# Norms on a row per head, another engine order and another transfer order ahead of a chunked recurrence

## The reference

```python
kk = heads(zk * k_k)
kk = kk / jnp.maximum(jnp.sqrt(jnp.sum(kk * kk, axis=-1, keepdims=True)), 1e-12)
k = zk * (1.0 + (a - 1.0) * k_a)
def step(state, inp):
    r_t, d_t, k_t, v_t, kk_t, a_t = inp
    sa = jnp.einsum('bhij,bhj->bhi', state, -kk_t)
    state = (state * d_t[:, :, None, :] + sa[..., None] * (kk_t * a_t)[:, :, None, :]
             + v_t[..., None] * k_t[:, :, None, :])
    return state, jnp.einsum('bhij,bhj->bhi', state, r_t)
...
mean = jnp.mean(y, axis=-1, keepdims=True)
var = jnp.mean(jnp.square(y - mean), axis=-1, keepdims=True)
y = ((y - mean) * lax.rsqrt(var + GN_EPS)).reshape(B, S, H * N)
```

## Time and profile before

| what | us |
|---|---|
| median of 3 runs | 1891.51 |
| lowest and highest run | 1888.94, 1892.16 |
| the profiled execution | 1893.17 |
| its span | 1891.4 |
| TensorE busy | 1767.9 |
| VectorE busy | 1201.5 |
| ScalarE busy | 791.1 |
| GpSimd busy | 178.5 |

### The profile page before, as it was taken

How to read it: one execution, slowest core, us unless ns; L and a number is a source line. 1 busy time by engine, 2 the same in 40 slices (tenths; PEclk the granted TensorE clock), 3 DMA queues, 4 the chain that set the end, 5 groups by cost and what they waited for, 6 DMA issues and landing times.

```text
span 1891.4 us, 29535 instructions
## 1 busy us (share of the span) xinstructions
PE 1767.9 (93%) x12770; PEld 1629.6 (86%) x12770; DVE 1201.5 (64%) x1828; ACT 791.1 (42%) x1131; POOL 178.5 (9%) x72
## 2 busy tenths in 40 slices
PE   6979979889989899999999999999999998999997
PEld 5869867789989899998898888888899898987897
DVE  5775665664688648875444998555575455555664
ACT  4624432434444432234443222444434545454553
POOL 0200321000555720000000000000000000000000
PEclk8889976899999999999999999999999998999999
DMA  9414232244435443335554333555654333443330
GB/s 380 178 67 166 103 112 94 107 156 156 157 137 198 157 155 113 112 112 191 187 179 156 112 112 112 200 190 189 249 180 165 128 144 129 150 151 126 112 112 23
DMA packets 40452, 281.70 MB, mean 149 GB/s; under 512 B 4481, under 2 KB 4865, under 8 KB 7938
## 3 DMA queue, kind: packets, MB, share of 16 engines
q1 hardware_dynamic: 40034, 279.66, 41.1%
q10 hardware_dynamic: 288, 0.15, 0.0%
HBM read 278.75 MB, written 1.05 MB: 148 GB/s over the span
## 4 chain that ended last, share of the span: by engine, by line
PE 81%; DVE 12%; ACT 3%; POOL 2%; DMA 1%; issue 1%; ACTq 0%; SPq 0%; DVEq 0%
PE ps L549 80%; POOL WL L2486 2%; DVE WL L1743 1%; DVE ar L1716 1%; DVE ar L2199 1%; DVE ar L1735 1%; DVE ar L2196 1%; DMA ar<-in_in_g 1%; ACT WH L1196 1%; ACT ar L1188 1%; DVE ar L2203 1%; DVE ar L2018 1%; DVE ar L1727 1%; DMA vec<-in_vec 0%; DVE ar L1892 0%
## 5 line engine op out<-in xcount | busy, mean ns | idle before, releaser
L549 PE MATMUL ps<-RH,WH 128*128 128x256 f32 x2520 | 745.5, 296 | 47.1 <-DVE WL L1743 16.1
L549 PE MATMUL ps<-RL,WH 128*128 128x256 f32 x2520 | 724.4, 287 | 0.0
L549 PE MATMUL ps<-RH,WL 128*128 128x256 f32 x2520 | 723.6, 287 | 0.0
L1743 DVE TENSOR_TENSOR WL<-ar,WH 128x1024 fp32r<-128x1024 f32 (+1 forms) x410 | 482.4, 1209 | 361.0 <-ACT WH L1196 360.8
L1196 ACT ACTIVATE WH<-ar 128x1024 fp32r<-128x1024 f32 (+1 forms) x478 | 480.1, 1040 | 308.2 <-PE ps L549 271.3
L549 PEld LDWEIGHTS ps<-RH,WH 128*128 128x128 f32 x2520 | 495.4, 197 | 62.3 <-issue 19.1
L549 PEld LDWEIGHTS ps<-RL,WH 128*128 128x128 f32 x2520 | 496.0, 197 | 2.9 <-issue 2.4
L549 PEld LDWEIGHTS ps<-RH,WL 128*128 128x128 f32 x2520 | 495.0, 196 | 0.0
L549 PE MATMUL ps<-ar 128*128 128x64 f32 (+10 forms) x2700 | 325.4, 300 | 33.9 <-DVE ar L1731 10.0
L549 PEld LDWEIGHTS ps<-ar 128*128 128x128 f32 (+6 forms) x2700 | 279.3, 185 | 75.1 <-issue 39.9
L549 PE MATMUL ps<-WH,RH 128*128 128x512 f32 (+1 forms) x704 | 262.5, 373 | 19.5 <-DVE WL L1743 12.7
(11 more groups left out here) (146 smaller groups left out, 1022.5 us busy)
## 6 DMA issues: line engine op xcount, KB each, us to landing
ar<-in_u SPq DMA_DIRECT2D x64, 1024.0 KB, 4.8
ar<-in_v SPq DMA_DIRECT2D x64, 1024.0 KB, 4.8
ar<-in_adr SPq DMA_DIRECT2D x16, 1024.0 KB, 4.8
ar<-in_ada SPq DMA_DIRECT2D x8, 1024.0 KB, 12.5
ar<-in_in_g SPq DMA_DIRECT2D x8, 1024.0 KB, 7.2
ar<-in_wq SPq DMA_DIRECT2D x8, 1024.0 KB, 4.8
ar<-in_a_qk SPq DMA_DIRECT2D x8, 1024.0 KB, 6.8
ar<-in_a_v SPq DMA_DIRECT2D x8, 1024.0 KB, 4.8
```

Source lines behind the costliest of these rows:

```text
L549: ins = q.matmul(o, l, r, start=start and i == 0, stop=stop and i == len(pairs) - 1, skip_group_check=skip)
L1743: q.tensor_tensor(l[:, x:z, :], src[:, x:z, :], h[:, x:z, :].bitcast(F32), ALU.subtract).then_inc(*v.up(("lo", n, i)))
```

## The change

1. **Norms on a row per head.** `head_sums` replaces `blksum` for kk and `y_sum` for the variance: for tile k the weights are every fourth column of `blk`, so the sums come out on 32 partitions, 32k to 32k + 31, the first 16 for one head, the other 16 for the other. All eight heads then lie in one tile of 128 x 256 (128 x 128 for half of the output). Bound, root and reciprocal work on that tile. `spread` then brings each head's number back to its 64 rows: a matmul with 32 rows of a new constant, two of them side by side in two waves, with a wait for the first wave. The products that apply the inverse read it from PSUM.
2. **Order of VectorE and ScalarE ahead of the solves.** The products with `k_k` on `al` come first, the norm's steps are taken apart and stand between the chunks' low halves, the key factors on ScalarE come after the root, sine and cosine move from there into the solves (steps 2 and 6 of the first half, with VectorE's part at step 4), the products by the inverse come after the first value chunks' low halves.
3. **Low halves** of `in_rkv` 4 and 5 are VectorE's.
4. **Transfers.** `dma_order` sorts the chunks from `in_v` 0 to `adr` 15 by when their slot comes free, in terms of the position of the chunk that holds it; `adr` chunks count as later. Slots stay as they were.

```diff
+def dma_order():
+    lo, hi = CHUNKS.index(("in_v", 0)), CHUNKS.index(("adr", 15)) + 1
+    def free(c):
+        return chunk_before(c) + (0.5 if CHUNKS[c][0] == "adr" else -1.5)
+    return list(range(lo)) + sorted(range(lo, hi), key=free) + list(range(hi, len(CHUNKS)))
...
-    return name == "in_g" or name == "in_rkv" and j >= 4 or name == "u" and j < 32 and j % 4 != 3
+    return name == "in_g" or name == "u" and j < 32 and j % 4 != 3
...
+    def head_sums(o, src, ts, need):
+        p.wait_ge(*on(need))
+        for k in range(4):
+            ins = mm(o[32 * k:32 * k + 32, 0:ts.stop - ts.start], [(blk[:, 0:P:4], src[:, k, ts])])
+        return ins
+    def spread(tag, rows, need):
+        w = rows.shape[1]
+        banks = [bank((tag, f)) for f in range(0, 4, 2)]
+        p.wait_ge(*on(need))
+        for g in range(2):
+            if g == 1:
+                p.wait_ge(*p.last())
+            for f, o in zip(range(0, 4, 2), banks):
+                s = slice(32 * (f + g), 32 * (f + g) + 32)
+                mm(o[:, g * w:(g + 1) * w], [(cst("spread")[s, :], rows[s, :])]).then_inc(*p.up((tag, f)))
...
-        blksum("kk norm", m.SQ, "kk squared")
+        head_sums(bank("kk norm"), m.SQ, slice(0, T), "kk squared").then_inc(*p.up("kk norm"))
+        some(zs, 8)
+        spread("kk inverse", m.kk, "kk inverses")
         finish(zs)
...
             if i == 11:
-                y_sum("y var", 0, m.Ysq, ("y squared", 0))
+                y_var(0)
+            if i == 13:
+                spread(("y inverse", 0), m.Yrt[0], ("y inverses", 0))
...
         some(steps, 2)
-        y_sum("y var", 1, m.Ysq, ("y squared", 1))
+        y_var(1)
+        some(steps, 4)
+        spread(("y inverse", 1), m.Yrt[1], ("y inverses", 1))
```

More of the change, by code:

```diff
@@ L1877, in front, with keyed @@
         some(zs, 7)
-        Bt, zr, zk = m.Bt, m.rd, m.zk
-        some(zs, 4)
-        for f in range(2):
-            t = ("kk norm", f)
-            v.wait_ge(*on(t))
-            q.tensor_scalar(flat(m.RN)[:, f * 512:(f + 1) * 512], tile(t), 1e-24, None, ALU.max).then_inc(*v.up("kk norm2"))
-            v.mark(("out", t))
+        zr, zk = m.rd, m.zk
+        some(zs, 3)
+        def keyed(x):
+            v.wait_ge(*v.last())
+            for k in range(4):
+                q.scalar_tensor_tensor(x[:, k, :], zk[:, k, :], vc("k_k", k), x[:, k, :], ALU.mult, ALU.mult).then_inc(*v.up())
+        v.wait_ge(*on("kk norm"))
+        TS(m.kk, tile("kk norm")[:, 0:T], 1e-24, None, ALU.max, None, "kk norm2")
+        v.mark(("out", "kk norm"))
+        v.wait_ge(*on(("out", ("sums before", 2))))
+        keyed(m.al)
+        some(zs, 2)
+        v.wait_ge(*on("kk norms"))
+        REC(m.kk, m.kk, "kk inverses")
+        some(zs, 4)
         v.wait_ge(*on("key factors"))
@@ L2615, in constants @@
     put("mask3", np.concatenate([tri, np.zeros((P, P)), tri], 1))
+    put("spread", row % 32 == col // 64 * 16)
     put("iota", col * np.ones((P, 1)))
```

75 lines of the change are left out of this document (44 added, 31 removed).

## The result

| | runs | median, us | lowest, highest |
|---|---|---|---|
| before | 4 | 1891.51 | 1888.94, 1892.16 |
| changed | 4 | 1875.63 | 1872.92, 1877.93 |

The ratio is 0.9918, with a 95% interval of 0.9901 to 0.9935: 15.9 us less, where 22.1 were forecast (1869.4, range 1858 to 1880). The profiled execution took 1876.42 (span 1874.6) against 1893.17 (1891.4): 16.8 us between the two traces. Direction and range held; most terms of the sum did not.

A forecast was written before the change was run, and what follows sets the result against it. TensorE, nearly always busy, was taken as the bound, so time comes only from its holes and low-clock stretches. 16.3 - 1.5 - 1.0 + 4.3 + 3.0 + 1.0 = 22.1 us, median 1869.4, range 1858 to 1880.

The forecast's parts named there:

- The front: Kernel start to TensorE's wait for VectorE's mask product at 133.05: VectorE sets that point at 116.6, 16.3 us earlier.
- first value chunk 100.5, a quarter of the second 102.0, solves at 102.3: TensorE's walked times ahead of the solves, which were to start at 102.3 us instead of 121.16.
- The signs of the later stages: Profile after: in_g 5 issued some 30 us early, no ScalarE transfer wait above 4 us, dot products 1.2 us each.
- The narrow norm: kk path ahead of the solves: head sums priced at 0.6 us, reciprocal of 256 columns 1.75, spread 1.5.
- The drain at a change of tiling: TensorE's short norm matmuls: none charged; at half of 1.07 us each, eight switches would make 18 instead of 22.
- Clock at the meeting point, -1.5: Where TensorE waits for VectorE's mask product near 116: idle of about 2.9 us may lower the clock, 1.5 us charged.
- Sine, -1.0: ScalarE's table load and two operations moved into the solves, ahead of a transposed tile's evacuation: loss of 1.0 us.
- Transfers, 7.3: Gate chunks issued ahead of adr rows: 4.3 us at the third head, 3.0 at the dot products and memset.
- The rival "worth nothing": Order of transfers gains nothing, another wait in the recurrence ends last: 14.8 us gained, to 1877; chance 0.17.
- Output norm, +1.0: Variance of the output: second half gains 1.4 us, first half costs TensorE 0.4, together 1.0 gained.
- half of the kk path's 1.5 and some 0.3, gives 1.1 back: Output norm's second half: spread on TensorE with hand-over costs 1.1 of the 2.5 us its shorter reciprocal saves.
- The rival "the front gives only part": Four kk-norm hand-offs stand in full queues, 2 us each, 8 us less: 14 gained, to 1877.5; chance 0.12.

The follow-up runs named there:

- The run with GpSimd: Changed kernel with the low halves of the last two rkv chunks back on GpSimd: 1875.09 us, ratio 0.9925.
- the free bank: Changed kernel with the first tile of the spread kk inverses in PSUM bank 7 instead of bank 6: 1869.79 us, ratio 0.9896.
- the two runs on this part alone: Changed kernel with the old transfer order: 1880.88 us, ratio 0.9958; kernel before with the new transfer order: 1880.33 us, ratio 0.9951.

## Why the prediction held, and where it did not

**The front, 16.3 forecast, 9.5 measured.** The step that failed is the line "first value chunk 100.5, a quarter of the second 102.0, solves at 102.3". It walked instructions and low halves, and not who holds which PSUM bank. The value chunk was ready at 95.3 and waited until 101.19 for a bank that VectorE's product at 100.36 frees; behind that idle its matmuls ran at 1.2 GHz; from there the second value chunk, ScalarE's next high half and the masks were all late. With another bank the front comes out at 43.4 us from the kk sums against 41.9 forecast, so the rest of the walk was short by 1.5, and by 1.4 to 3.1 in the other four traces with that bank.

Two of the signs named beforehand say the same. The solves were to start no later than 110, and a TensorE hole above 3 us was not to stand between 75 and 120: they start at 111.64, and the hole is 5.87. The signs of the later stages came: dot products of 1.21 us at 237.67, no wait for a gate chunk, no hole at the third head, the last early gate chunk 25 us ahead of its use ("some 30").

**The narrow norm.** The prices were right: head sums 0.67 us (0.6 taken), reciprocal 1.75, spread 1.50 (1.5 taken). As built the form was worth nothing to the front, since its bank cost at least what the reciprocal saved.

**The drain at a change of tiling.** The Trainium skill (TensorEngine Tiling (Array Packing), Key Properties) says that such a change drains TensorE. I had weighed half of 1.07 us for each. The head sums leave no room for that: half of the eight matmuls in the row at 19.16 are 0.54 us, and they take 0.67, so 0.13 is left where two switches would be 1.07. The spread's 1.50 us hold a wait between two waves, and no run parts that from a switch.

**GpSimd's low halves.** Right in kind: VectorE's products returned to 2.48 and 1.67 us. The run with GpSimd puts this part at some 2 us of the front, in one trace.

**Clock at the meeting point, -1.5.** TensorE idles 0.54 us there, not 2.9. That it came late with the bank is not the whole reason: with the free bank it is 0.56, since TensorE waits 0.89 and 0.33 us for VectorE shortly before. The clock stays at 1.00 across the point in both, so the term had no object there. A low clock came instead behind the hole that the forecast did not have, and cost 2.4 us up to the start of the solves.

**Sine, -1.0.** Wrong in sign. From the meeting point to the next common mark both kernels take 9.83 us, so nothing was lost where the sines went; and where they stood they would have cost 2.6. I priced the place they moved to and not the hand-offs they left.

**Transfers, 7.3.** Right as a mechanism: the two places, the holes and waits that go. The lead grew by 12.5 us from the end of the solves to the first variance in the first pair of traces; the two runs on this part alone give 5 to 9 us of time. The rival "worth nothing" falls.

**Output norm, +1.0.** Minus 1 to 2, by the stretches of four traces with the old norm and seven with the new. The step that failed is "half of the kk path's 1.5 and some 0.3, gives 1.1 back": it left out that TensorE idles for the reciprocal and that the spread stands in TensorE's queue where VectorE must wait for it.

**What the sum left out.** The same program behind the hole ahead of `wo` takes up to 5.8 us more or less from trace to trace, and the changed kernel took 190.3 and 185.5 us from the meeting point to the first variance. That is as large as most terms above, and a forecast to within 5 us on this kernel needs luck. The rival "the front gives only part" named the right stage and size (14, 1877.5) with the wrong mechanism.

## What to carry to other kernels

When an operation gets a new result tile, walk the buffers as well as the queues: who takes that bank next, and on which engine's last read its release hangs. A short operation put into a full queue costs its position, not its duration, so look at who waits on each side. Marks made of holes with equal length and cause tell real leads from what the clock adds, and where a stretch of small work runs at the low clock, filler work given earlier (9.6 us by the medians) helped as much as the largest waits taken out of it (5 to 9 us).

## What the runs showed of the hardware

- The granted clock's answer to one and the same idle (2.17 us before the same matmul) differs from execution to execution: 1.00 in two traces, 0.89 over the 20 us behind it in one. The common last 1496 us differ by up to 5.8 us between traces, and go with the time at 1.2 GHz, 51 to 72 us.
- Behind the idle of 5.87 us the granted clock was 0.50 from 101.2 to 105 us; without that idle it was 1.00 there, and the same work up to the solves took 8.02 us instead of 10.45.
- Four matmuls of 32 weight columns by 256, one on each quarter of the columns, take 0.67 us; four with 32 rows of weights by 256, in two waves, 1.50 us.
- A reciprocal on VectorE goes by its columns: 0.95 us for 128, 1.75 for 256, 3.35 for 512, 6.55 for 1024.
